# mLSTM and its output stage in one loop, on one NeuronCore

## The reference, cut to what matters

```
proj = rms(x) @ w_in_3            # columns qx, zx, xm, om, zm
xc   = silu(causal_conv(xm))
q, k = blockdiag(xc), blockdiag(xc);  v = blockdiag(xm);  i, f = gates(q, k, v)
a[s] = i[s] - cumsum(logsigmoid(f))[s]
M[t] = max over s <= t of max(a[s], ...)
D[s,t] = exp(a[s] - M[t]) for s <= t, else 0
h[t]   = sum_s D[s,t] (q[t].k[s]/16) v[s] / max(|sum_s D (q.k)/16|, exp(-m[t]))
h    = head_norm(h * sigmoid(om)) * g_head
y    = (h + skip * xc) * silu(zm)
x    = x + y @ w_out_3[that part];  out = rms(x) * g_final
```

## Time and profile before

| | us |
|---|---|
| median of 3 runs | 4386.75 |
| the profiled execution | 4389.42 |
| its span, first to last instruction | 4387.6 |
| mean granted clock of TensorE | 0.935 |
| PE busy (with its weight loads apart) | 3901.0, 89% |
| DVE busy | 2231.2, 51% |
| ACT busy | 946.3, 22% |
| POOL busy | 423.3, 10% |

### The profile page before, as it was taken

One profiled execution on the slowest core, in us unless ns is written; L12 is line 12 of the kernel. 1 busy time (PEld: TensorE's weight loads), 2 busy tenths in 40 slices (PEclk: granted clock), 3 DMA queues, 4 the chain that ended last, 5 costly groups with the idle time before them and its releaser, 6 DMA issues. The chain is left out here.

```text
span 4387.6 us, 44584 instructions
## 1 busy us (share of the span) xinstructions
PE 3901.0 (89%) x17747; PEld 3068.2 (70%) x17747; DVE 2231.2 (51%) x2954; ACT 946.3 (22%) x1823; POOL 423.3 (10%) x178
## 2 busy tenths in 40 slices
PE   8999879999998799876799999979999998798818
PEld 6665668888876587676588888857777776653716
DVE  6565485556574739677454444453223221542573
ACT  1455210000011511321400000030122223212331
POOL 0112023232310014121000000000000000000010
PEclk9998889999998899888899999989999999898959
DMA  4100112222222111200211111121111114211020
GB/s 143 30 20 20 67 49 108 72 102 78 100 84 78 60 39 39 82 1 1 77 39 38 57 42 54 69 95 39 56 69 52 70 53 158 69 48 39 1 101 39
DMA packets 123743, 267.35 MB, mean 61 GB/s; under 512 B 11504, under 2 KB 25924, under 8 KB 123588
## 3 DMA queue, kind: packets, MB, share of 16 engines
q1 hardware_dynamic: 123588, 265.22, 16.8%
HBM read 220.11 MB, written 45.09 MB: 60 GB/s over the span
## 5 line engine op out<-in xcount | busy, mean ns | idle before, releaser
L130 PE MATMUL banks<-region_parts 128*128 128x512 f32 x3354 | 1338.6, 399 | 108.1 <-DVE weight_chunks_parts L124 98.7
L130 PEld LDWEIGHTS banks<-region_parts 128*128 128x128 f32 x3354 | 635.7, 190 | 284.6 <-issue 85.5
L132 PE MATMUL banks<-region_parts,weight_chunks_parts 128*128 128x512 f32 x2112 | 829.9, 393 | 0.0
L131 PE MATMUL banks<-weight_chunks_parts,region_parts 128*128 128x512 f32 x1984 | 778.8, 393 | 0.0
L132 PE MATMUL banks<-region_parts 128*128 128x512 f32 x1696 | 664.6, 392 | 0.0
L131 PE MATMUL banks<-region_parts 128*128 128x512 f32 x1658 | 651.0, 393 | 0.0
L132 PEld LDWEIGHTS banks<-region_parts,weight_chunks_parts 128*128 128x128 f32 x2112 | 400.6, 190 | 85.3
L131 PEld LDWEIGHTS banks<-weight_chunks_parts,region_parts 128*128 128x128 f32 x1984 | 377.0, 190 | 81.7 <-issue 5.3
L132 PEld LDWEIGHTS banks<-region_parts 128*128 128x128 f32 x1696 | 320.6, 189 | 67.6
L131 PEld LDWEIGHTS banks<-region_parts 128*128 128x128 f32 x1658 | 314.8, 190 | 65.4 <-issue 2.4
L554 ACT ACTIVATE region<-gain_offset 128x512 f32<-128x512 f32 x128 | 81.0, 633 | 1272.1 <-DVE gain_offset L502 1272.1
(11 more groups left out here) (368 smaller groups left out, 5075.5 us busy)
## 6 DMA issues: line engine op xcount, KB each, us to landing
weight_chunks<-in_w_in SPq DMA_DIRECT2D x19, 2048.0 KB, 8.3
weight_chunks<-in_w_up SPq DMA_DIRECT2D x16, 2048.0 KB, 8.4
weight_chunks<-in_w_down SPq DMA_DIRECT2D x16, 2048.0 KB, 7.8
extra<-in_w_ada SPq DMA_DIRECT2D x16, 1536.0 KB, 11.0
x_spill<-region SPq DMA_DIRECT2D x32, 512.0 KB, 10.7
weight_chunks<-in_w_out SPq DMA_DIRECT2D x8, 2048.0 KB, 8.2
region<-x_spill SPq DMA_DIRECT2D x32, 512.0 KB, 9.8
f_spill<-region SPq DMA_DIRECT2D x64, 256.0 KB, 2.0
```

The lines of the kernel that those rows point to most:

```text
L130: pe.matmul(out, m.parts(lhs[0]), m.parts(rhs[0]), start=first, stop=False)
L131: pe.matmul(out, m.parts(lhs[0]), m.parts(rhs[1]), start=False, stop=False)
L132: return pe.matmul(out, m.parts(lhs[1]), m.parts(rhs[0]), start=False, stop=last)
```

## The change

The stage `mlstm_out` is gone; its work stands in the loop of `mlstm`, and with it come these edits:

- In `dilated_attention` the om groups leave the bank through Tanh of half the value (a sigmoid up to a factor), the zm groups through Tanh and a VectorE operation that makes twice Silu out of it and releases the bank.
- In `attention_out` ScalarE also writes `skip * xc` to two staging buffers, and that is stored in place of `xc`. VectorE, not ScalarE, waits for the last stores.
- In the loop a fifth state buffer: the new state goes to the spare one, and the old one becomes the spare. The values are gated straight from the bank (`gated`), undivided; the denominator goes into the variance (`variances`, `shifts`), the norm is one ScalarE operation (`norm`), six units behind; TensorE turns the normed head seven units behind (`turn_h`), ScalarE writes it with the gain (`head`). Per token tile VectorE adds the skip, multiplies by z and makes the low part (`skip`, `close`, `y_to_low`), ScalarE the high part. The first weight chunk is split in units 24 to 28. The mask moves into the cap: the table holds bounds of -3e38 and 3e38 in place of ones and zeros.
- TensorE waits for the split of a token tile only, ahead of the product of that tile, and turns the last seven heads among the first three products. SP loads the skip and z parts by token tile.

```diff
-                    act.activation(stage[n % 2], m.bank[:, 6 + n % 2, :], ACT.Copy).then_inc(staged, 1)
-                    act.wait_ge(staged, n + 1)
-                    act.sem_inc(wt.bank_free, 1)
+                    if n >= SILU:
+                        act.activation(stage[n % 2], m.bank[:, 6 + n % 2, :], ACT.Tanh, scale=0.5).then_inc(half_open, 1)
+                    else:
+                        if n >= GATE:
+                            ins = act.activation(stage[n % 2], m.bank[:, 6 + n % 2, :], ACT.Tanh, scale=0.5)
+                        else:
+                            ins = act.activation(stage[n % 2], m.bank[:, 6 + n % 2, :], ACT.Copy)
+                        ins.then_inc(staged, 1)
+                        act.wait_ge(staged, n + 1)
+                        act.sem_inc(wt.bank_free, 1)
...
+            def silu(n):
+
+                dve.wait_ge(half_open, n - SILU + 1)
+                dve.scalar_tensor_tensor(stage[n % 2], stage[n % 2], 1.0, m.bank[:, 6 + n % 2, :], op0=ALU.add,
+                                         op1=ALU.mult).then_inc(staged, 1)
+                dve.wait_ge(staged, n + 1)
+                dve.sem_inc(wt.bank_free, 1)
...
+                if SILU < n <= NG:
+                    silu(n - 1)
...
                 act.activation(xc[k], xc[k], ACT.Silu).then_inc(s.xc_ready, 1)
+                act.wait_ge(s.xc_ready, k + 1)
+                if k >= 2:
+                    act.wait_ge(s.spilled[k % 2], 16 * (k // 2))
+                act.activation(m.gb[:, k % 2, :], xc[k], ACT.Copy, scale=m.c("skip", k)).then_inc(s.sx_ready, 1)
+            act.wait_ge(s.sx_ready, NK)
             for n, k in enumerate(order):
-                act.wait_ge(s.spilled, 16 * NK)
...
+            for b in range(2):
+                dve.wait_ge(s.spilled[b], 16 * NK // 2)
...
-    C = [room(2 * EC).rearrange("p (c e) -> p c e", e=EC) for _ in range(M_HEADS)]
+    C = [room(2 * EC).rearrange("p (c e) -> p c e", e=EC) for _ in range(M_HEADS + 1)]
...
+            def load_sx(j):
+                sp.dma_start(sx[j % 2], a.sx_spill.rearrange("k p n -> p k n")[:, :, j * P:(j + 1) * P]).then_inc(s.sx_in[j % 2], 16)
+
+            def load_z(j):
+                z = a.f_spill[48:64].rearrange("(k b) p n -> b p k n", b=2)[j // 4][:, :, (j % 4) * P:(j % 4 + 1) * P]
+                for n in range(2):
+                    sp.dma_start(z_of(j, n), z[:, 4 * n:4 * n + 4, :]).then_inc(s.z_in[j % 2], 16)
+            sp.wait_ge(s.turned_m, 1)
+            for j in range(2):
+                load_sx(j)
+            for j in range(NT):
+                if j >= 2:
+                    sp.wait_ge(s.skipped, j - 1)
+                    load_sx(j)
+                    sp.wait_ge(s.y_ready, j - 1)
+                sp.wait_ge(s.gated, M_HEADS * (j + 1))
+                load_z(j)
+            sp.wait_ge(s.av, N)
...
+            def turn_h(u):
+                j, h = units[u]
+                pe.wait_ge(s.normed, u + 1)
+                if u >= IN_LOOP + 4:
+                    pe.wait_ge(s.headed, u - 3)
+                elif u >= IN_LOOP + 2:
+                    pe.wait_ge(s.gated, N)
+                elif u >= IN_LOOP:
+                    pe.wait_ge(s.state, NU)
+                for c in range(2):
+                    mm = pe.transpose(turn_place(u, c), v[:, 2 * h + c, j * P:(j + 1) * P], m.ident)
+                mm.then_inc(s.h_turned, 1)
...
-                    pe.wait_ge(s.h_ready, n - 1)
+                    pe.wait_ge(s.gated, n - 1)
...
+            def products(c, g):
+                G = wt.outs
+                pe.wait_ge(wt.bank_free, G + 1)
+                for kk in range(NK):
+                    mm = split_products(m, pe, m.bank[:, G % NBANK, :], [t[:, kk, g * P:(g + 1) * P] for t in (y_high, y)],
+                                        [t[:, kk, :] for t in (w_high[c], m.wbuf[:, (n0 + c) % 2])], kk == 0, kk == NK - 1)
+                mm.then_inc(wt.mm_done, 1)
+                wt.outs += 1
+            pe.wait_ge(s.headed, N - TURN)
+            pe.wait_ge(s.w_split, 4)
+            tail = list(range(N - TURN, N))
+            for g in range(NT):
+                for u in tail[:3] if g in (0, 1) else tail[:1] if g == 2 else []:
+                    turn_h(u)
+                tail = tail[3:] if g in (0, 1) else tail[1:]
+                pe.wait_ge(s.y_split, g + 1)
+                products(0, g)
+            wt.used += 1
+            pe.wait_ge(m.split_done, split0 + 1)
+            for g in range(NT):
+                products(1, g)
+            wt.used += 1
 
...
+            def norm(u):
+                j, h = units[u]
+                act.wait_ge(s.shifted, j + 1)
+                x = pair(v, h, j)
+                act.activation(x, x, ACT.Identity, scale=rstd[:, j % 2, h:h + 1], bias=shift[:, j % 2, h:h + 1]).then_inc(s.normed, 1)
...
+            def after(n):
+                if n >= M_HEADS + 1 and n % M_HEADS == 1:
+                    roots(n // M_HEADS - 1)
+                if NORM <= n < N + NORM:
+                    norm(n - NORM)
+                if TURN <= n < N + TURN:
+                    head(n - TURN)
+                if n >= 14 and n % M_HEADS == 2:
+                    y_to_high((n - 14) // M_HEADS)
+                if 24 <= n < 28:
+                    w_to_high(n - 24)
             for n in range(N + 1):
...
-                dve.tensor_scalar(capped[n % 2], Gb[:, h, j * P:(j + 1) * P],
-                                  ac[:, 4 * j + h:4 * j + h + 1], None, ALU.max).then_inc(s.capped, 1)
+                dve.scalar_tensor_tensor(capped[n % 2], Gb[:, h, j * P:(j + 1) * P], ac[:, 4 * j + h:4 * j + h + 1], bound,
+                                         op0=ALU.max, op1=ALU.max).then_inc(s.capped, 1)
...
-                m.dve_link(dve, dve.tensor_tensor(d, d, upto, ALU.mult))
...
-                    dve.wait_ge(s.av, n + 1)
-                    dve.scalar_tensor_tensor(C[h], C[h], decay[:, 4 * j + h:4 * j + h + 1], new, op0=ALU.mult,
-                                             op1=ALU.add).then_inc(s.state, 1)
+                    dve.wait_ge(s.av, n)
+                    dve.scalar_tensor_tensor(C[held[n]], C[held[n - M_HEADS]], decay[:, 4 * j + h:4 * j + h + 1], new,
+                                             op0=ALU.mult, op1=ALU.add).then_inc(s.state, 1)
...
+                x, d = pair(v, h, j), dd[:, j % 2, h:h + 1]
+                m.dve_link(dve, dve.tensor_scalar(d, bank[:, 2 * P:EC], -1.0, em[:, 4 * j + h:4 * j + h + 1], ALU.mult, ALU.max))
+                m.dve_link.n += 1
+                dve.tensor_tensor(d, d, bank[:, 2 * P:EC], ALU.max).then_inc(m.dve_link.sem, 1)
+                dve.scalar_tensor_tensor(x, gate_of(j, h), 1.0, bank[:, 0:2 * P].rearrange("p (c n) -> p c n", n=P),
+                                         op0=ALU.add, op1=ALU.mult).then_inc(s.gated, 1)
+                dve.wait_ge(s.gated, n + 1)
+                m.dve_link.n += 1
+                dve.bn_stats(bn[:, j % 2, h], x).then_inc(m.dve_link.sem, 1)
...
+            def variances(j):
+
+                b = j % 2
+                dve.wait_ge(m.dve_link.sem, m.dve_link.n)
+                if j >= 2:
+                    dve.wait_ge(s.normed, M_HEADS * (j - 1))
+                for h in range(M_HEADS):
+                    m.dve_link.n += 1
+                    dve.bn_aggr(mv[:, b, h], bn[:, b, h]).then_inc(m.dve_link.sem, 1)
+                m.dve_link(dve, dve.reciprocal(dd[:, b], dd[:, b]))
+                m.dve_link(dve, dve.tensor_tensor(vv[:, b], mv[:, b, :, 1], dd[:, b], ALU.mult))
+                m.dve_link(dve, dve.tensor_tensor(vv[:, b], vv[:, b], dd[:, b], ALU.mult))
+                dve.tensor_scalar(vv[:, b], vv[:, b], 1e18, 4 * RMS_EPS, ALU.min, ALU.add).then_inc(s.var_ready, 1)
...
+            def skip(j):
+
+                dve.wait_ge(s.headed, M_HEADS * (j + 1))
+                dve.wait_ge(s.sx_in[j % 2], 16 * (j // 2 + 1))
+                dve.tensor_tensor(tile(y, j), tile(y, j), sx[j % 2], ALU.add).then_inc(s.skipped, 1)
+
+            def close(j):
+
+                dve.wait_ge(s.skipped, j + 1)
+                dve.wait_ge(s.z_in[j % 2], 32 * (j // 2 + 1))
+                for n in range(2):
+                    part = tile(y, j)[:, 4 * n:4 * n + 4, :]
+                    ins = dve.scalar_tensor_tensor(part, part, 0.5, z_of(j, n), op0=ALU.mult, op1=ALU.mult)
+                    if n == 0:
+                        m.dve_link.n += 1
+                        ins.then_inc(m.dve_link.sem, 1)
+                        dve.wait_ge(m.dve_link.sem, m.dve_link.n)
+                ins.then_inc(s.y_ready, 1)
+
+            def y_to_low(j):
+                dve.wait_ge(s.y_high, j + 1)
+                low_part(m, dve, tile(y_high, j), tile(y, j)).then_inc(s.y_split, 1)
+
...
+            def rest(n):
+
+                if n >= M_HEADS and n % M_HEADS == 0:
+                    variances(n // M_HEADS - 1)
+                if n >= M_HEADS + 1 and n % M_HEADS == 1:
```

(41 more changed lines are left out.)

298 lines of the change are left out of this document (120 added, 178 removed).

## The result

The changed kernel takes 4263.4 us, the median of its runs (4255.47 to 4263.55), against 4385.67 beside it for the kernel before. The ratio is 0.9716 (95% interval 0.9696 to 0.9735), so 122 us less. Run again on another chip it took 4260.4 (5 runs, ratio 0.9708, 0.9695 to 0.9721). One further run was left out: its granted clock was 0.55 throughout and its time 6624. The profiled execution took 4263.55 us, 125.9 less than that of before, with a span of 4261.8.

What follows compares the result with a forecast made beforehand. It took the output stage to be bound by phases one behind another and the loop by a ring of values and state update. Terms -116.9 + 0.7 - 1.9 = -118.1 gave 4268.7, plus 2.3 for small waits: 4271 us, range 4258 to 4297.

Steps and rivals of the forecast that it cites:

- The spare state buffer: mLSTM loop: updating into a spare buffer lets VectorE's update run beside the values, removing TensorE's 0.74 us gap per unit.
- TensorE in a unit: mLSTM loop: 3.69 us active plus two transposes of the normed head at 0.26, so 3.95 us from unit 7 on.
- VectorE in a unit: mLSTM loop: 2.76 us per unit plus 1.35 for once-per-tile pieces, 4.11 us where TensorE needs 3.95.
- The rule against it: VectorE in the loop: waiting out each printed duration would cost 0.08 us more per operation, a unit some 5.1 us.
- The loop: mLSTM loop with the output stage inside: 124.5 us, last values at 4169.7 against 4170.2 before.
- Tail, POOL, SP: Last tiles' work beside the first products, POOL's removed z product and SP's 24 loads: all costed at zero.
- Inside the product: Products: seven pairs of transposes +1.8 us, clock loss 2 after the gap in place of 3.1; together +0.7.
- The conv stage: Stage before the loop: ScalarE's last scaled copy costs 1.1 us, the spill wait of 3.1 goes; gain 1.9.
- TensorE alone sets the pace: Rival, loop: VectorE's pieces shorter than costed, units at 3.95 us, clock does not fall; 4263 us, chance 0.10.
- VectorE's queue becomes a real bound: Rival, loop: each wide piece exposes a wait or drain, unit 4.8 to 5.1 us; 4290 us, chance 0.22.
- The uncovered tail: Rival, loop's end: products catch up with tiles 5 to 7, TensorE stops up to 15 us; 4286 us, chance 0.05.
- The serial ring: Rival, loop: TensorE, VectorE and ScalarE run one after another, unit 10.7 us; 4450 us, chance 0.03.

Runs made afterwards that it cites:

- b_both: Kernel before, with the spare state buffer and VectorE's state update ahead of the division, output stage untouched; 4363.98 us, ratio 0.9957.
- b_spare: Kernel before, with the spare state buffer alone, order of VectorE's queue unchanged; 4385.71 us, ratio 1.0002.
- b_order: Kernel before, with VectorE dividing behind the state update, state still in place; 4372.73 us, ratio 0.9971.
- tail_early_again: Changed kernel, repeat run with only two of the tail's heads turned before the first product, then three, then two; 4253.82 us, ratio 0.9692.
- after_again: Changed kernel run once more, unedited, on another chip; 4260.4 us, ratio 0.9708.
- after: Changed kernel itself, its first run and profile; 4263.4 us, ratio 0.9716.
- a_inplace: Changed kernel with the state updated in place again, order kept; 4269.4 us, ratio 0.9743.
- a_dve_dose: Changed kernel with the statistics of each unit made twice on VectorE; 4276.4 us, ratio 0.9743.
- a_wait_all: Changed kernel with TensorE waiting for the split of all eight token tiles before the first product; 4276.58 us, ratio 0.9747.
- a_skip_pool: Changed kernel with the skip sum of a token tile on POOL in place of VectorE; 4275.72 us, ratio 0.9754.

## Why the prediction was right, and where its steps were not

The predicted 4271 stands 7.6 us above the measured 4263.4, which is inside the range and just under the forecast's own 4264 to 4279. The working, step by step:

*What bounds the kernel: right.* The 119 us of the output stage were phases in a string. From the start of the loop to the first product it is now 116.9 us in place of 245.4, 128.5 less: 26.0 because the ring is open (`b_both`), minus 14.4 for the output stage's work inside the loop (113.4 against 99.0), plus 116.9 for the stage itself (3.5 in place of 120.3). The saving comes from TensorE running on, not from fewer operations.

*The spare state buffer: wrong in its cause.* "The 0.74 us gap is gone" came true for the change, but the step gave it to the buffer alone. `b_spare` shows nothing for it, `b_order` 13 us for the order, `b_both` 26. And while the weights are split TensorE does wait for the state update again (1.04 and 1.14 us), a gap that the prediction's signs ruled out; there VectorE comes late with all of its work. The row for it was in sight: in the earlier trace rows the state update follows a denominator that waits 1.98 us for the values. I followed the semaphore and not the queue in front of it.

*TensorE in a unit: 3.95 predicted, 3.67 to 3.70 measured.* The step took as active all that was not a printed wait, 4.43 - 0.74. But behind a wait the engine needs longer too: from the scores to the state product it was 1.35 us, 0.61 without the wait, and 0.44 in `b_both`; the state product's first pair took 0.50 and now 0.44. So 3.45 was really active. The two transposes cost their 0.25 on top of that, and are not free.

*VectorE in a unit: 2.76 + 1.35 = 4.11 predicted, 3.80 measured* (15.18 per tile). The unit shown above without its skip of 1.12 is 3.70 - 1.12 = 2.58. The gate (0.45) and statistics (0.35) were right; the weights cost 0.20, for which I had taken a duration of 0.29, because no next start stood behind it in the earlier trace rows; the cap 0.26. What is left, 3.80 - 2.58 = 1.22 a unit or 4.9 a tile, answers to my 5.4.

*The rule against it.* From start to start the state costs 0.66 us at a duration of 0.74 and the skip 1.12 at 1.21, so the next operation starts 0.08 us before the printed end, as in the rows of before. The Trainium skill's rule (VectorE: DVE Perf Modes, The DRAIN you can't avoid), read as a wait for the printed end, would have given a unit of 5.1 us. The trace disagrees with that reading.

*The loop: 124.5 predicted, 113.4 measured.* First three units 7.7 for 8.6, the next three 10.6 for 11.1, four 14.7 for 15.8, then seventeen with the weights 67.8 for 75.4, the last four 12.6 for 13.6. Most of it is the two mis-sized units above. The last four units were sized too high by themselves: one of the four quarters of the weights fell among them, so without it they took 11.5 for 13.6. The loop is the one large miss of the sum, 11 us, and with it two of the signs were missed: a unit of 4.0 to 4.2, and last values near 4170 (they end at 4160.84).

*The gap from loop to product: 4.0 predicted, 4.07 measured* (4160.84 to 4164.91). `tail_early_again` shows that it was not needed.

*Tail, POOL, SP: right at zero.* Tile 5's parts are ready 5.1 us behind the first product (5), the last tile's 19.4 (17), the second chunk's split 27.3 (25), all before their turn. TensorE waits for nothing among the products, and no engine in the loop waits for a transfer.

*Inside the product: +0.7 predicted, -0.2 measured.* The turns' 1.8 and a loss of clock are there in the first profile: matmuls take 0.63 us in place of 0.40 until 4169. In `after_again`, after the same 3.39 us wait, they take 0.39 from the start and the products 88.3. The same stretch in both, busy time and granted clock, `after` first:

```profile
4165.00:4169.00 4.00, 4.00 (x13) 3.10 (x12) 2.19 (x4) 3.59 (x8) 0.00 (x0) 0.60 0.44 129
```
```profile
4165.00:4169.00 4.00, 3.73 (x18) 3.12 (x19) 2.18 (x4) 4.00 (x10) 0.00 (x0) 1.00 0.34 92
```

In `a_inplace`, behind a wait of 3.39 us too, the clock was 0.50 for the first 5 us and the products took 90.9. So the loss of clock behind such a gap is 0 in one execution, about 1.6 in the second and 2.6 in the third, inside the 0 to 3 of the prediction.

*The conv stage: 1.9 predicted, about 1.1 measured.* ScalarE's timeline of the changed kernel, last Silu and first q copy:

```profile
3901.81 1.06 ACT L1896 ACTIVATE extra<-extra 128x1024 f32<-128x1024 f32 x1 [8.63 <-DVE extra L1930]
3902.90 1.15 ACT L1900 ACTIVATE gain_offset<-extra,columns 128x1024 f32<-128x1024 f32 x1
3905.15 0.60 ACT L1906 ACTIVATE region<-banks 128x512 f32<-128x512 f32 x1 [1.11 <-PE banks L1866]
```

From the Silu to the copy it is 3.34 us now, 4.15 before, so the copy comes 0.8 earlier and not 2; the wait for the stores went, and TensorE's products came late in its place. The gate rows follow 105.05 us behind the Silu, before 106.12.

*The projection stage: right at zero.* It ends 1.62 us later than before (3673.61 against 3671.99), but VectorE's third unit is already 1.68 late (3159.64 against 3157.96), ahead of the first edited copy. ScalarE's groups in 3140 to 3672:

```profile
L1541 ACT ACTIVATE region<-banks 128x512 f32<-128x512 f32 x32 | 19.1, 597 | 118.5 <-PE banks L132 118.5
...
L1524 ACT ACT_TABLE_LOAD x1 | 1.3, 1283 | 1.7 <-PEq L3151 1.7
```

Exp and Tanh alternate there with one table load in the whole stage. That agrees with the Trainium skill (ScalarE: Activation LUTs, Table sets: the hidden batching unit), by which both are in one set.

*The start of the loop: -1.9 predicted, +2.8 measured.* In this trace the 1.62 us are there from the start, and ScalarE waits 17.07 us, not 13.15, for the first load of the cross attention, 5.5 late together; at the last Silu the lag is 3.8, and the conv stage takes 1.1 off. The starts of the thirteen profiled executions above spread wider than this, so I take it for scatter; why a load lands earlier in one and later in another stays open.

*The rivals.* The measured 4263.4 is the number of "TensorE alone sets the pace", but its mechanism holds for units 3 to 10 only; from there `a_dve_dose` shows VectorE. "VectorE's queue becomes a real bound" was right in the engine and wrong in the price: full, but up to the weights' units without an exposed wait behind it. The uncovered tail is excluded by `a_wait_all`, which also prices it at 14.7 us where I had up to 15. The serial ring is excluded by the unit of 3.80, far from 8.4. That 11 us too much for the loop meets 4.7 too little ahead of it makes the total look better than its terms, and that is luck.

## What to carry to other kernels

When a buffer is added to open a ring, look at what stands in front of the freed instruction on its in-order engine: if that waits for the same producer, the buffer gives nothing until the order changes as well. Take an engine's active time from a stretch in which it doesn't wait, since the latency behind a wait counts as work otherwise, and take costs from start to start. A serial stage is best paid by dealing its pieces out to the units of a loop before it, up to the point where one engine is full; `tail_early_again`, at 4253.8 us the version to keep, is 6.6 below the changed kernel, of which the trace shows 3.8 for not putting a late piece ahead of ready work.

## What the runs showed of the hardware that was not expected

- A POOL sum of 128x1024 in float32 (2.35 us) holds up a VectorE operation that reads two tiles in SBUF until the sum has ended: 2.45 to 2.48 in place of 0.35 for one of only 128x128, in each of the five tiles where the two met. Operations with one tile from SBUF, beside the same sum, kept their 0.41 and 0.43. The Trainium skill (SBUF — State Buffer, Who interferes with whom) has the lock between a VectorE instruction with two SBUF inputs and a GpSimd instruction that reads SBUF; the rows agree, and add the size.
- After one and the same wait of TensorE (3.39 us) the granted clock was 0.60 over the next 4 us in one profiled execution (0.63 us a matmul), 0.50 over 5 us in another kernel's, and 1.00 in a third (0.39). In `a_skip_pool` the same wait of 1.96 us was followed by a low clock twice and by a full one the third time.
- The start of the loop, 4050 us into the kernel, moved by up to 17 us between executions of the same code ahead of it, while the loop repeated to a tenth of a microsecond (113.4 in five traces).
